# Four transformer layers and a fifth block on one core: eight more up-projection chunks per layer in the wide form, and the gate-value product issued behind the next chunk's additions

## The chip, the cores and the metric

The kernel runs on one core of a Trainium2 chip. TensorE (PE) multiplies, with its weight loads shown apart (PEld); VectorE (DVE), ScalarE (ACT) and GpSimd (POOL) do the elementwise work; SyncE (SP) issues the transfers of the weights. The metric is the device time of one execution in microseconds (us), lower is better.

## The reference

All of it is in float32 on a sequence of 256 tokens with 1024 channels. Four layers have an attention (three kinds) and a gated feed-forward network with a causal convolution of width 3 on both halves of the hidden tensor. A fifth block has another mixer and a network whose convolution is on the gate half alone.

```python
def conv_gated_ffn(h, w_up, conv_w, conv_b, w_down):      # layers 0 to 3, D_FF = 2752
    u = h @ w_up
    u = lax.conv_general_dilated(u, conv_w[:, None, :], ..., padding=[(CONV_W - 1, 0)],
                                 feature_group_count=C) + conv_b
    gate, val = jnp.split(u, 2, axis=-1)
    return (jax.nn.silu(gate) * val) @ w_down

def conv_ffn(h, w_up, conv_w, conv_b, w_down):            # the fifth block, D_FF_2 = 2816
    gate, val = jnp.split(h @ w_up, 2, axis=-1)
    ...                                                   # convolution of width 3 on gate
    return (jax.nn.gelu(conv, approximate=True) * val) @ w_down
```

## The kernel before

**Splitting for precision.** A matmul operand is kept as two parts of the type fp32r, high and low. A product is made of three: high weight by high activation, high weight by low activation, low weight by high activation. In `h_both` and `act_both` the high and the low part of an activation tile lie side by side (256 columns each).

**Weights.** SyncE brings the weights in 241 pieces of 1 MB (128 x 2048) into the three buffers of `w_raw` (line 392); piece n+3 is issued once the low part of piece n is made. ScalarE writes the high part into one of five slots, `w_hi` (the cast of line 411), and VectorE the low part, `w_lo` (the subtraction of line 957). A chunk of the up projection uses one piece. TensorE waits for the low part of its chunk's piece (`lo_ready`) and for its banks (`bank_free`).

**The up stage.** It has 22 chunks, numbered 0 to 21; a chunk makes 128 gate channels (bank `pj[slot]`) and 128 value channels (bank `val_bank[slot]`) for all 256 tokens, with three slots that are used in turn, so that TensorE can start chunk c+3 once the banks of chunk c are free. Chunks 0 to 2 follow the norm of the layer and are made in a form of their own. From chunk 3 on a chunk is *narrow* or *wide* (table `WIDE_UP`, line 73):

- narrow: per channel tile and per 128 input channels three matmuls of 256 columns (lines 1787 to 1789), 48 in a chunk, all summed in columns 0 to 255 of the bank;
- wide: one matmul of the low weight by 256 columns (line 1799) and one of the high weight by high and low activation together, 512 columns (line 1802), 32 in a chunk. The part of the low activation ends up in columns 256 to 511 of the bank, and the two halves have to be added.

Chunks 10 to 19 of layers 0 to 3 are wide, and chunks 2 to 21 of the fifth block. Chunk 21 of layers 0 to 3 has half the channels (`half_step`).

**The work behind a chunk**, in the order in which each engine issues it, narrow chunk j of layers 0 to 3:

- ScalarE: two activations that start the convolution, scale and bias, from the banks to `cgate` and `cval` (slices of `tmp`, line 890); the high part of the piece of chunk j+4 or j+5 (line 411); silu of the gate (line 894), which waits for three of VectorE's taps.
- VectorE: four taps of the convolution (line 1544), `tmp` plus a weight times a shifted source; the low part of a piece (line 957), of chunk j+3 up to chunk 3, of chunk j+4 from chunk 4 on, so that chunk 4 has two of them; the product of gate and value (line 1564), which waits for the silu.
- GpSimd: the cast of the product to the high part of `act_both` (line 1759) and the subtraction that leaves the low part (line 1762).

In a narrow chunk the taps read the bank. In a wide chunk ScalarE first copies the right halves of both banks to `tmp` (line 875), VectorE adds them to the left halves into `u_sb` (line 1536, two additions; the second frees the banks), and the activations and taps read `u_sb`. In the fifth block there is one activation, two taps, and the product is on line 1569.

**The down stage** begins on TensorE with the hidden tiles 0 to 18 of its first two output tiles, 76 matmuls, for which those tiles must be ready; then it waits for all hidden tiles and for a cast of ScalarE (line 907) that moves the half tile 21 to where the matmul needs it. The half tile comes from VectorE's product of line 1493 and GpSimd's cast and subtraction behind it.

Of the kernel before, what the change touches and what calls it, by code (L numbers as in the profile page):

```python
# [37 lines left out]
FT = 22  # L38
RING = 3
# [32 lines left out]
RAW = 3  # L72
WIDE_UP = (range(10, 20),) * 4 + (range(2, FT),)
UNITS = STD // P
# [25 lines left out]
def build(nc, xT, w_std, params, consts, lam, onehot, tables, pT, out):  # L100
    ctx = ExitStack()
    with ctx:
# [67 lines left out]
        bank_free = sem("bank_free")  # L170
# [114 lines left out]
        def wide_count(ffn, j):  # L285

            return sum(len(WIDE_UP[f]) for f in range(ffn)) + j - WIDE_UP[ffn][0] + 1

# [30 lines left out]
        def slot_of(c0, k):  # L319
            return (c0 + k) % RING  # L320
# [624 lines left out]
        def _(dve):  # L945
# [291 lines left out]
            for kind, c0, n in STAGES:  # L1237
# [188 lines left out]
                elif kind == "wo":  # L1426
# [54 lines left out]
                    app += 1  # L1481
                elif kind == "up":
                    def half_step(j, c, slot):
                        at = j * 8 + PARAM["conv"] + ffn * FT * 8
                        dve.wait_ge(conv_init, (j + ffn * FT) * 2 + 2)
                        dve.scalar_tensor_tensor(cgate[:, slot, 1:S], pj[slot][:, 0:S - 1], par[:, at + 1:at + 2],
# [9 lines left out]
                    def step(j, c, slot, split):  # L1496
# [45 lines left out]
                        def tap(v, lag):  # L1542
# [4 lines left out]
                                ALU.mult, ALU.add)  # L1547

                        for v in range(convs):
                            dve.wait_ge(conv_init, init + (v + 1))  # L1550
                            tap(v, 1).then_inc(conv_part, 1)
# [5 lines left out]
                        split()  # L1557
                        dve.wait_ge(gated, n_ + 1)
                        if convs == 2:
                            if wide:  # L1560
                                dve.wait_ge(wide_taps, wide_count(ffn, j))
                            else:
                                dve.wait_ge(bank_free, c + (RING + 1))
                            dve.tensor_tensor(cval[:, slot, :], cgate[:, slot, :], cval[:, slot, :],  # L1564
                                              ALU.mult).then_inc(prod_done, 1)
                        else:
                            if wide:
# [4 lines left out]
                            else:  # L1572
                                product.then_inc(bank_free, 1)
                                dve.wait_ge(bank_free, c + (RING + 1))
                                dve.memset(wait_mark[:, 0:1], 0.0).then_inc(prod_done, 1)

                    for j in range(n):
                        step(j, c0 + j, slot_of(c0, j), lambda: split_to(weights_of(layer, c0 + j) + low_up(j)))
                    ffn += 1
                elif kind == "down":  # L1580
# [1005 lines left out]
```

## Time and profile before

| | us |
|---|---|
| median of 3 runs | 1475.66 |
| lowest, highest | 1474.86, 1477.33 |
| profiled execution, its own time | 1474.86 |
| its span in the trace | 1472.9 |

Share of the span in which each engine is busy: PE 100%, PEld 92%, DVE 76%, ACT 63%, POOL 23%. The granted TensorE clock is at its full level in all forty slices of the page. A busy span of TensorE overstates its work, since matmuls overlap; for the length of a stretch the starts of its matmuls are to be read, and what could hold it up is to be read on the other engines. In a timeline, instructions of one line are merged: the second number is the time from the start of the first to the end of the last.

### The profile page before, as it was taken

What the parts mean: (1) busy time and instruction counts of PE and PEld (TensorE: products, weight loads), DVE (VectorE), ACT (ScalarE), POOL (GpSimd) and SP (SyncE); (2) the same over time, 40 slices, a digit from 0 to 9 for tenths busy, and PEclk for the clock granted to TensorE, in tenths of its full rate; (3) what the DMA queues carried; (4) which work ended last, traced back from release to release, by engine and by line L of the source; (5) the groups of instructions that cost most, each with busy time, mean ns of one, the idle gap of its engine ahead of it and who ended that gap; (6) DMA issues with size and microseconds to landing.
All of it is one profiled execution on the core that took longest, in us unless ns stands there. A gap on an engine that the chain in (4) does not pass through costs nothing.

```text
span 1472.9 us, 26512 instructions
## 1 busy us (share of the span) xinstructions
PE 1466.7 (100%) x10440; PEld 1357.9 (92%) x10440; DVE 1119.5 (76%) x1885; ACT 926.6 (63%) x1536; POOL 331.5 (23%) x461
## 2 busy tenths in 40 slices
PE   9999999999999999999999999999999999999998
PEld 8999989899999898989989899999898999988888
DVE  7778898565578995787899566688995688798655
ACT  7776666456756674575676456766664558566453
POOL 2104212211132222212322221023212271022100
PEclk9999999999999999999999999999999999999999
DMA  8644656444335565562565546545655464356560
GB/s 277 202 165 138 222 197 223 168 162 162 115 134 206 204 204 196 175 199 79 204 206 199 199 159 198 160 134 210 204 196 193 165 213 175 109 206 206 176 222 32
DMA packets 39687, 265.03 MB, mean 180 GB/s; under 512 B 5247, under 2 KB 5562, under 8 KB 8976
## 3 DMA queue, kind: packets, MB, share of 16 engines
q1 hardware_dynamic: 36432, 255.54, 49.9%
q0 software_dynamic: 2992, 7.79, 2.2%
q8 instruction: 82, 1.34, 0.4%
q14 instruction: 37, 0.30, 0.1%
q10 hardware_dynamic: 144, 0.05, 0.0%
HBM read 262.24 MB, written 1.12 MB: 179 GB/s over the span
## 4 chain that ended last, share of the span: by engine, by line
PE 98%; ACT 1%; DVE 1%; DMA 1%; issue 0%; SPq 0%; ACTq 0%
PE bank L1802 29%; PE bank L1799 14%; PE bank L1787 13%; PE bank L1788 13%; PE bank L1789 13%; PE bank L1850 6%; PE bank L1859 3%; PE bank L2034 1%; PE bank L2023 1%; PE bank L2015 1%; PE bank L2014 1%; DMA w_raw<-w_std 1%; PE bank L2394 1%; PE bank L2035 1%; PE bank L2087 0%; PE bank L2209 0%
## 5 line engine op out<-in xcount | busy, mean ns | idle before, releaser
L957 DVE TENSOR_TENSOR w_lo<-w_raw,w_hi 128x2048 fp32r<-128x2048 f32 x239 | 549.5, 2307 | 74.4 <-ACT w_hi L411 74.3
L411 ACT CAST w_hi<-w_raw 128x2048 fp32r<-128x2048 f32 x239 | 452.7, 1903 | 82.7 <-DMA w_raw<-w_std 62.4
L1802 PE MATMUL bank<-h_both,w_hi 128*128 128x512 f32 x960 | 301.5, 395 | 0.0
L1787 PE MATMUL bank<-h_both,w_hi 128*128 128x256 f32 x992 | 284.3, 287 | 0.0
L1788 PE MATMUL bank<-h_both,w_hi 128*128 128x256 f32 x992 | 280.6, 283 | 0.0
L1789 PE MATMUL bank<-h_both,w_lo 128*128 128x256 f32 x992 | 280.5, 283 | 0.0
L1802 PE MATMUL bank<-act_both,w_hi 128*128 128x512 f32 x848 | 267.4, 395 | 0.0
L1799 PEld LDWEIGHTS bank<-h_both,w_lo 128*128 128x128 f32 x960 | 179.9, 188 | 42.4 <-DVE w_lo L957 0.3
L1787 PEld LDWEIGHTS bank<-h_both,w_hi 128*128 128x128 f32 x992 | 189.9, 191 | 4.0 <-issue 2.8
L1788 PEld LDWEIGHTS bank<-h_both,w_hi 128*128 128x128 f32 x992 | 190.0, 192 | 0.4
L1789 PEld LDWEIGHTS bank<-h_both,w_lo 128*128 128x128 f32 x992 | 190.0, 192 | 0.0
L1799 PE MATMUL bank<-h_both,w_lo 128*128 128x256 f32 x960 | 188.7, 278 | 0.0
L1799 PEld LDWEIGHTS bank<-act_both,w_lo 128*128 128x128 f32 x848 | 157.2, 188 | 34.2
L1799 PE MATMUL bank<-act_both,w_lo 128*128 128x256 f32 x848 | 170.1, 278 | 0.0
L1759 POOL CAST act_both<-tmp 128x256 f32 x110 | 53.9, 490 | 438.4 <-DVE tmp L1564 319.3
L1802 PEld LDWEIGHTS bank<-h_both,w_hi 128*128 128x128 f32 x960 | 146.2, 189 | 0.0
L1802 PEld LDWEIGHTS bank<-act_both,w_hi 128*128 128x128 f32 x848 | 130.7, 189 | 1.7
L1544 DVE SCALAR_TENSOR_TENSOR tmp<-u_sb,par,tmp 128x255 f32<-128x255 f32 x234 | 115.4, 536 | 21.7 <-ACT tmp L890 20.9
L1850 PE MATMUL bank<-h_both,w_hi 128*128 128x256 f32 x400 | 106.8, 289 | 0.2 <-DVE w_lo L1143 0.2
L1850 PE MATMUL bank<-h_both,w_lo 128*128 128x256 f32 x400 | 104.5, 283 | 0.0
L1787 PE MATMUL bank<-act_both,w_hi 128*128 128x256 f32 x340 | 99.2, 292 | 0.0
L1788 PE MATMUL bank<-act_both,w_hi 128*128 128x256 f32 x340 | 96.1, 283 | 0.0
(236 smaller groups left out, 2549.7 us busy)
## 6 DMA issues: line engine op xcount, KB each, us to landing
w_raw<-w_std SPq DMA_DIRECT2D x239, 1024.0 KB, 4.9
act_both<-vec_dram POOLq DMA_DIRECT2D x56, 128.0 KB, 3.4
w_raw<-w_std SPq DMA_DIRECT2D x3, 512.0 KB, 8.5
x<-xT SPq DMA_DIRECT2D x2, 512.0 KB, 5.5
out<-x SPq DMA_DIRECT2D x3, 256.0 KB, 2.1
w_raw<-w_std SPq DMA_DIRECT2D x2, 256.0 KB, 4.9
par<-params SPq DMA_DIRECT2D x1, 446.0 KB, 6.6
cst<-consts SPq DMA_DIRECT2D x1, 256.0 KB, 9.4
```

The source lines that it names most:

```text
L411: act.copy(w_hi[:, n % SLOTS, :], w_raw[:, n % RAW, :]).then_inc(hi_ready, 1)
L957: dve.tensor_tensor(w_lo[:, n % SLOTS, :], w_raw[:, n % RAW, :], w_hi[:, n % SLOTS, :].bitcast(F32), ALU.subtract).then_inc(lo_ready, 1)
L1544: return dve.scalar_tensor_tensor(to[:, slot, lag:S], source(v)[:, 0:S - lag], par[:, bass.ds(at + (4 * v + 2 - lag), 1)], to[:, slot, lag:S],
L1759: pool.tensor_copy(act_hi[:, bass.ds(j, 1), :].squeeze(1) if not isinstance(j, int) else act_hi[rows, j, :], cval[rows, slot, :]).then_inc ...
L1787: pe.matmul(dst, wh, xh, start=first, stop=False, skip_group_check=shared)
L1788: pe.matmul(dst, wh, xl, start=False, stop=False, skip_group_check=shared)
L1789: done = pe.matmul(dst, wl, xh, start=False, stop=last, skip_group_check=shared)
L1799: pe.matmul(bank[:, 0:S], weights[k][1], moving[k][0], start=start and k == 0, stop=False, skip_group_check=True)
L1802: done = pe.matmul(bank[:, :], weights[k][0], moving[k][1], start=False, stop=stop and k == len(weights) - 1, skip_group_check=True)
L1850: pe.matmul(dst, a, b, start=k == 0 and w is wh and (n == 0 or not shared), stop=False, skip_group_check=shared)
L1859: done = pe.matmul(dst, a, b, start=False, stop=k == DT - 1, skip_group_check=shared)
L2014: pe.matmul(into[m][:, 0:QB], q[:, 0:QB], k[:, 0:QB], start=True, stop=True)
```

## The change

The table makes chunks 3 to 9 and chunk 20 of layers 0 to 3 wide too (18 wide chunks a layer, where there were 10), and the product of chunk j is no longer issued on VectorE at the end of chunk j but in chunk j+1, behind the scaling of a first chunk or the two additions of a wide one and ahead of the taps. The last one is issued ahead of the half chunk's taps, or after the stage. This holds for all chunks of layers 0 to 3 and for chunk 0 and the wide chunks of the fifth block. ScalarE's and GpSimd's code is as it was; what a wide chunk needs there follows from the table.

```diff
-WIDE_UP = (range(10, 20),) * 4 + (range(2, FT),)
+WIDE_UP = (range(3, FT - 1),) * 4 + (range(2, FT),)
...
                 elif kind == "up":
+                    later = []
+
+                    def multiply_later():
+
+                        if later:
+                            later.pop()()
+
                     def half_step(j, c, slot):
                         at = j * 8 + PARAM["conv"] + ffn * FT * 8
+                        multiply_later()
                         dve.wait_ge(conv_init, (j + ffn * FT) * 2 + 2)
...
+                        multiply_later()
                         for v in range(convs):
                             dve.wait_ge(conv_init, init + (v + 1))
                             tap(v, 1).then_inc(conv_part, 1)
...
                         split()
-                        dve.wait_ge(gated, n_ + 1)
-                        if convs == 2:
...
+                        def multiply():
+
+                            dve.wait_ge(gated, n_ + 1)
+                            if convs == 2:
+                                if wide:
+                                    dve.wait_ge(wide_taps, wide_count(ffn, j))
+                                else:
+                                    dve.wait_ge(bank_free, c + (RING + 1))
+                                dve.tensor_tensor(cval[:, slot, :], cgate[:, slot, :], cval[:, slot, :],
+                                                  ALU.mult).then_inc(prod_done, 1)
+                                return
...
+                        if convs == 2 or first or wide:
+                            later.append(multiply)
+                        else:
+                            multiply()
+
                     for j in range(n):
                         step(j, c0 + j, slot_of(c0, j), lambda: split_to(weights_of(layer, c0 + j) + low_up(j)))
+                    multiply_later()
```

VectorE's instructions in layer 0 from the taps of chunk 3 to the product of chunk 4, before (L1544 are the taps, L957 the low part of a weight piece, L1564 the product):

```order
226 L1544 SCALAR_TENSOR_TENSOR tmp<-bank,par,tmp 128x255 x2
227 L1544 SCALAR_TENSOR_TENSOR tmp<-bank,par,tmp 128x254 x2
228 L957 TENSOR_TENSOR w_lo<-w_raw,w_hi 128x2048
229 L1564 TENSOR_TENSOR tmp<-tmp 128x256
230 L1544 SCALAR_TENSOR_TENSOR tmp<-bank,par,tmp 128x255 x2
231 L1544 SCALAR_TENSOR_TENSOR tmp<-bank,par,tmp 128x254 x2
232 L957 TENSOR_TENSOR w_lo<-w_raw,w_hi 128x2048 x2
233 L1564 TENSOR_TENSOR tmp<-tmp 128x256
```

The same place in the changed kernel, from the additions of chunk 3 to the two low parts of chunk 4 (there L1544 are the additions, L1576 the product, L1552 the taps):

```order
225 L1544 TENSOR_TENSOR u_sb<-bank,tmp 128x256 x2
226 L1576 TENSOR_TENSOR tmp<-tmp 128x256
227 L1552 SCALAR_TENSOR_TENSOR tmp<-u_sb,par,tmp 128x255 x2
228 L1552 SCALAR_TENSOR_TENSOR tmp<-u_sb,par,tmp 128x254 x2
229 L957 TENSOR_TENSOR w_lo<-w_raw,w_hi 128x2048
230 L1544 TENSOR_TENSOR u_sb<-bank,tmp 128x256 x2
231 L1576 TENSOR_TENSOR tmp<-tmp 128x256
232 L1552 SCALAR_TENSOR_TENSOR tmp<-u_sb,par,tmp 128x255 x2
233 L1552 SCALAR_TENSOR_TENSOR tmp<-u_sb,par,tmp 128x254 x2
234 L957 TENSOR_TENSOR w_lo<-w_raw,w_hi 128x2048 x2
```

Two additions have come in, the taps read `u_sb` and `tmp` instead of a bank and `tmp`, and the product (of the chunk before) stands between the additions and the taps.

VectorE at the end of the stage, from the taps of chunk 20 to the last low part ahead of the down stage, before (L1486 and L1489 are the half chunk's taps, L1493 its product):

```order
304 L1544 SCALAR_TENSOR_TENSOR tmp<-bank,par,tmp 128x255 x2
305 L1544 SCALAR_TENSOR_TENSOR tmp<-bank,par,tmp 128x254 x2
306 L957 TENSOR_TENSOR w_lo<-w_raw,w_hi 128x2048
307 L1564 TENSOR_TENSOR tmp<-tmp 128x256
308 L1486 SCALAR_TENSOR_TENSOR tmp<-bank,par,tmp 128x255
309 L1489 SCALAR_TENSOR_TENSOR tmp<-bank,par,tmp 128x254
310 L957 TENSOR_TENSOR w_lo<-w_raw,w_hi 128x2048
311 L1493 TENSOR_TENSOR tmp<-tmp 64x256
312 L957 TENSOR_TENSOR w_lo<-w_raw,w_hi 128x2048
```

And in the changed kernel (L1494, L1497 and L1501 for the half chunk):

```order
310 L1544 TENSOR_TENSOR u_sb<-bank,tmp 128x256 x2
311 L1576 TENSOR_TENSOR tmp<-tmp 128x256
312 L1552 SCALAR_TENSOR_TENSOR tmp<-u_sb,par,tmp 128x255 x2
313 L1552 SCALAR_TENSOR_TENSOR tmp<-u_sb,par,tmp 128x254 x2
314 L957 TENSOR_TENSOR w_lo<-w_raw,w_hi 128x2048
315 L1576 TENSOR_TENSOR tmp<-tmp 128x256
316 L1494 SCALAR_TENSOR_TENSOR tmp<-bank,par,tmp 128x255
317 L1497 SCALAR_TENSOR_TENSOR tmp<-bank,par,tmp 128x254
318 L957 TENSOR_TENSOR w_lo<-w_raw,w_hi 128x2048
319 L1501 TENSOR_TENSOR tmp<-tmp 64x256
320 L957 TENSOR_TENSOR w_lo<-w_raw,w_hi 128x2048
```

From the product of chunk 20 on the order is the same as before; ahead of it the additions and the product of chunk 19 have come in.

## Rows read from the trace of the kernel before

**Rows 1.** Page, chain of work that ended last: share of the span by engine.

```profile
PE 98%; ACT 1%; DVE 1%; DMA 1%; issue 0%; SPq 0%; ACTq 0%
```

**Rows 2.** Timeline, TensorE, layer 0: start us, duration us, instruction; chunks 3, 10, 20 begin.

```profile
141.01 0.28 PE L1787 MATMUL bank<-h_both,w_hi 128*128 128x256 f32 x1
...
181.33 0.40 PE L1799 MATMUL bank<-h_both,w_lo 128*128 128x256 f32 x2
...
237.07 0.28 PE L1787 MATMUL bank<-h_both,w_hi 128*128 128x256 f32 x1
```

**Rows 3.** Timeline, VectorE, layer 0: chunk 4 (narrow), chunks 8 to 9 (narrow), chunk 10 (wide).

```profile
158.93 1.71 DVE L1544 SCALAR_TENSOR_TENSOR tmp<-bank,par,tmp 128x255 f32<-128x255 f32 x4
160.57 4.48 DVE L957 TENSOR_TENSOR w_lo<-w_raw,w_hi 128x2048 fp32r<-128x2048 f32 x2
...
178.32 0.42 DVE L1564 TENSOR_TENSOR tmp<-tmp 128x256 f32<-128x256 f32 x1
...
182.42 0.42 DVE L1564 TENSOR_TENSOR tmp<-tmp 128x256 f32<-128x256 f32 x1
...
187.51 0.76 DVE L1536 TENSOR_TENSOR u_sb<-bank,tmp 128x256 f32<-128x256 f32 x2 [0.58 <-ACT tmp L875]
188.61 1.76 DVE L1544 SCALAR_TENSOR_TENSOR tmp<-u_sb,par,tmp 128x255 f32<-128x255 f32 x4 [0.34 <-ACT tmp L890]
190.29 2.29 DVE L957 TENSOR_TENSOR w_lo<-w_raw,w_hi 128x2048 fp32r<-128x2048 f32 x1
```

**Rows 4.** Timeline, ScalarE: chunks 3 and 10 of layer 0, then chunk 3 of layer 1.

```profile
156.23 1.91 ACT L411 CAST w_hi<-w_raw 128x2048 fp32r<-128x2048 f32 x1 [3.59 <-DMA w_raw<-w_std]
158.04 0.41 ACT L894 ACTIVATE tmp<-tmp 128x256 f32<-128x256 f32 x1
...
187.11 0.65 ACT L875 COPY tmp<-bank 128x256 f32<-128x256 f32 x2 [1.47 <-PE bank L1802]
...
456.68 1.91 ACT L411 CAST w_hi<-w_raw 128x2048 fp32r<-128x2048 f32 x1 [4.78 <-DMA w_raw<-w_std]
```

**Rows 5.** Timeline of layer 1, a wide chunk: VectorE, then GpSimd.

```profile
503.60 0.41 DVE L1564 TENSOR_TENSOR tmp<-tmp 128x256 f32<-128x256 f32 x1
503.93 0.74 DVE L1536 TENSOR_TENSOR u_sb<-bank,tmp 128x256 f32<-128x256 f32 x2
505.01 1.94 DVE L1544 SCALAR_TENSOR_TENSOR tmp<-u_sb,par,tmp 128x255 f32<-128x255 f32 x4 [0.34 <-ACT tmp L890]
506.88 2.28 DVE L957 TENSOR_TENSOR w_lo<-w_raw,w_hi 128x2048 fp32r<-128x2048 f32 x1
...
504.18 0.40 POOL L1759 CAST act_both<-tmp 128x256 f32 x1 [4.17 <-DVE tmp L1564]
504.76 0.74 POOL L1762 TENSOR_TENSOR act_both<-tmp,act_both 128x256 f32 x1 [0.18 <-POOL act_both L1759]
```

**Rows 6.** Timeline, VectorE and GpSimd, two other places where both work from SBUF.

```profile
142.50 2.28 DVE L957 TENSOR_TENSOR w_lo<-w_raw,w_hi 128x2048 fp32r<-128x2048 f32 x1
...
144.70 2.14 DVE L1544 SCALAR_TENSOR_TENSOR tmp<-u_sb,par,tmp 128x255 f32<-128x255 f32 x4
...
142.69 2.69 POOL L1762 TENSOR_TENSOR act_both<-tmp,act_both 128x256 f32 x1 [0.19 <-POOL act_both L1759]
...
311.88 1.85 DVE L1003 SCALAR_TENSOR_TENSOR tmp<-x,par,rstd 128x256 f32<-128x256 f32 x2
...
311.35 2.09 POOL L1652 TENSOR_TENSOR h_both<-tmp,h_both 128x256 fp32r<-128x256 f32 x2 [16.50 <-ACT h_both L461]
```

**Rows 7.** Timeline, end of layer 0's up stage: VectorE, GpSimd, ScalarE, TensorE.

```profile
247.46 0.41 DVE L1564 TENSOR_TENSOR tmp<-tmp 128x256 f32<-128x256 f32 x1
...
251.91 2.40 POOL L1759 CAST act_both<-tmp 64x256 fp32r<-64x256 f32 x1 [2.55 <-DVE tmp L1493]
...
255.15 0.40 ACT L907 CAST act_both<-act_both 64x256 fp32r<-64x256 f32 x1 [3.39 <-POOL act_both L1762]
...
258.94 0.40 PE L1799 MATMUL bank<-act_both,w_lo 128*128 128x256 f32 x2
```

More of the change, by code:

```diff
@@ L1557, in step @@
                         split()
-                        dve.wait_ge(gated, n_ + 1)
-                        if convs == 2:
[L1560 to L1566, printed above, removed]
+                        def multiply():
[8 more added lines that the diff above has]
+                                return
                             if wide:
```

## The prediction, on record before the changed kernel ran

> **What bounds the kernel now.** I read the chain of waits first: 98% of it is TensorE [rows 1], so a change gains what it takes off TensorE and loses what it makes TensorE wait for. Then the starts of the matmuls in layer 0's up stage: chunks 3 to 9, narrow, last from 141.01 to 181.33, 5.76 us each; chunks 10 to 19, wide, from 181.33 to 237.07, 5.574 us each [rows 2]. A wide chunk is 0.186 us shorter.
>
> Next the engines behind it. In a narrow chunk VectorE needs 4.10 us where nothing makes it wait (product to product, 178.32 to 182.42 [rows 3]); TensorE needs 5.76. This spare 1.66 us a chunk is used: the stage starts with a backlog. TensorE ends chunk 4 at 141.01 + 2 x 5.76 = 152.5, VectorE takes it up at 158.93 [rows 3], 6.4 us later. At chunk 10 the backlog is gone: TensorE ends it at 186.90 (181.33 + 5.574), ScalarE copies at 187.11 [rows 4], VectorE adds at 187.51 [rows 3]. So **the narrow chunks are where VectorE catches up**, and they are what the change removes.
>
> **The gain on TensorE.** Eight chunks by 0.186 us is 1.49 us a layer, 5.95 us in four layers, as long as VectorE, ScalarE and the weights keep pace.
>
> **VectorE's time for a wide chunk, without GpSimd.** First addition to first tap 1.10 us (187.51 to 188.61), four taps 1.68 us to the start of the low part (190.29) [rows 3]; the low part 2.20 us to the next instruction (two take 4.48, one 2.28 [rows 3, 5]). Together 4.98. The product (0.33 us from its start to the next, 503.60 to 503.93 [rows 5]) came on top before and now falls into the wait of 0.34 us ahead of the first tap. By this sum the moved product saves 0.33 us, and a backlog would shrink by 0.6 us a chunk.
>
> **What the moved product runs into.** GpSimd starts on a product 0.58 us after it starts (504.18), and subtracts 0.58 us later (504.76), for 0.74 us [rows 5]. Three places show that such an instruction and a VectorE instruction with both inputs in SBUF don't run together. In layer 1 the first tap of a wide chunk comes during the subtraction, and the taps need 1.87 us (505.01 to 506.88 [rows 5]) instead of 1.68. In rows 6 a subtraction that begins 0.19 us into a low part lasts 2.69 us: the low part ends at 144.78, the subtraction at 145.38, 0.60 later; the four taps behind it span 2.14 us, against 1.71 for four that read a bank [rows 3]. And at 311.88 two taps of the norm's kind take 1.85 us together while GpSimd has two subtractions: GpSimd gets in between two VectorE instructions that stand back to back [rows 6]. Additions and narrow taps read a bank, and the narrow taps stand where GpSimd's work on the chunk before falls, yet take 1.71 [rows 3]; I count them as spared.
>
> Before, the 1.9 us after a product fell on additions and a wait (wide) or on bank taps (narrow). Now the product stands 0.67 us behind the first addition, so the cast comes at +1.25 and the subtraction at +1.83 to +2.6, and the four taps at +1.10 to +2.8: **both meet SBUF taps in every wide chunk**. The cast lies beside the first tap and delays the second by about 0.03 us. The subtraction gets in at a boundary between taps, keeps the port for 0.60 us, and the tap behind it ends 0.28 us after it (144.70 + 0.96 where the subtraction ended at 145.38; that 0.28 is my estimate from the two spans in rows 6); two taps that start 0.40 us apart are then 0.92 apart: +0.52. A wide chunk takes VectorE 4.98 + 0.55 = **5.53 us**, against TensorE's 5.574. Bounds: 4.98 if nothing collides, 5.7 if both get in separately and fully (0.26 + 0.52). I take 5.53, the value by rows 5 and 6. At 5.53 a backlog of 8 us stays for the whole stage.
>
> The Trainium skill, "SBUF — State Buffer", in the section with the single rule on ports, says that VectorE and GpSimd share one pair of SBUF ports as an exclusive lock: an instruction of VectorE with two SBUF inputs and one of GpSimd that reads SBUF block each other for their whole length. Rows 5 and 6 agree. By its "whoever starts first keeps it" alone, a subtraction could cost the taps its full 0.74 us, some 0.2 more a chunk than I take.
>
> **The backlog at the start.** In layer 0 ScalarE casts at 156.23, as before, since that waits for a transfer; it is issued behind the low part of chunk 2, which moves little. Silu of chunk 3 at 158.04 [rows 4], copies of chunk 4 at 158.35, additions 0.40 behind (187.11 to 187.51) at 158.75, first tap 159.85, the two low parts from 162.1 to 166.5 (1.68 + 0.55, then 2 x 2.20). The low part for chunk 7 is ready at 162.1 + 2.28 = 164.4; TensorE, 4 x 5.574 after 141.01, wants it at 163.3. So it **waits 1.1 us at chunk 7**, which eats most of the 1.49. Additions of chunk 5 at 166.5.
>
> **The end of the stage.** 15 chunks later, 15 x 5.53 = 83.0, additions of chunk 20 at 249.5; its product, now behind its low part, 5.53 later at 255.0. Before, that product was at 247.46 and the last cast ended at 255.15 + 0.40 = 255.55, 8.1 us later, with the same instructions between [rows 7]. I add 0.1 for a subtraction caught behind a low part: 255.0 + 8.2 = 263.2. TensorE needs this cast for hidden tiles 19 to 21; it took them up at 258.94 without a wait [rows 7], 3.4 us of cover. Now it starts them at 263.2: **+4.2 us in layer 0**, with the gain and the wait at chunk 7 in it, since this end is set by VectorE alone. On the way the down stage also begins late, as tile 18's product waits for chunk 19's additions; that wait is inside the 4.2.
>
> Layers 1 to 3 have the same program and the same start, so 4 x 4.2 = 16.8. In the fifth block only the product moves; two taps, then a low part, and VectorE has time there; I count -0.1 for a product less ahead of chunk 7. **Sum: +16.7 us.** The profiled execution took 1474.86 (span 1472.9); against the median 1475.66 that gives **1492.4 us**, +1.1%.
>
> One unknown: in layer 1 the cast of rows 4 stands at 456.68, 1.3 us later, counted from chunk 3, than in layer 0. Before, the narrow chunks absorbed it. Now such a late piece moves VectorE's whole stage: +1.2 us in each layer that has one, 0 to 4.8 in all. I count none, and put it in the range.
>
> **Rivals.**
> (a) *No collision that matters*: GpSimd's work finds room beside the taps or is held behind the low part. VectorE 5.0 us a chunk, the backlog is gone by chunk 20, gain 1.49 less 0.5 at chunk 7 or nothing: -1.0 to -1.5 a layer, **1470 us**. For it: the moved product does fill a real wait. Against it: three places in the rows. Faster.
> (b) *Half of it*: VectorE at 5.3. The end comes 15 x 0.23 = 3.4 us earlier, +0.8 a layer, **1479 us**. The point from which the sign turns is 5.25 us a chunk.
> (c) *Late pieces in the first chunks of most layers*, or 5.6 us a chunk: **1497 to 1500 us**. TensorE's clock stays at its level by the page; a wait of 3 us in each layer might change that, and I have no row for it.
> (d) *ScalarE, not VectorE, is late*: by rows 4 the copies take 0.65, a cast 1.91 and the silu 0.41, and the scaling between copies and first tap is shorter than the 1.10 between addition and tap [rows 3]: at most 4.1 of 5.57, so I give it nothing of its own.
>
> **How the numbers follow.** Forecast 64%, (a) 10%, (b) 13%, (c) 13%. The forecast's own spread, 4.2 ± 0.8 a layer, is 1489 to 1496. The range takes in half of (b) and most of (c): 1481 to 1498. This kernel's measurement tells 0.2% (3 us) from no change: faster 0.10 by (a); same 0.06, the low part of (b); slower 0.84.
>
> **What would show it.** In the changed profile: wide chunks on TensorE at 5.57 us; a gap of about 1 us at chunk 7; VectorE with additions 5.5 us apart from chunk 5 to 20, never waiting for the copies; one of the last three taps near 1 us long in each chunk; taps from `u_sb` with a mean well over 0.48; a wait of TensorE for ScalarE's cast of line 907, near 3 us in four places, and about 1 us at the start of the down stage. The prediction is wrong if taps stay at 0.48 us, or if VectorE waits for the copies in the middle of the stage.

## The result

The changed kernel takes 1501.22 us (median of 5 runs, 1500.75 to 1502.49), the kernel before 1475.66: ratio 1.0174, 95% interval 1.0163 to 1.0185. It is slower, as forecast, but by 26 us instead of 16.7, and outside the range of 1481 to 1498. The ratios below leave out one slow execution each of the kernels no_defer (7300.79 us) and defer_only (2889.83 us), which the medians given for these two include (without them 1496.15 and 1475.78 us).

### The profile page after: what moved, and what is told of

It is laid out like the page before. It is cut to its first block, busy times and chain, and to the rows that moved or that the text cites. A ratio compares the mean times of both kernels' runs of the same rounds, so it can differ in the third digit from the quotient of the medians.

```text
span 1499.6 us, 25616 instructions
## 1 busy us (share of the span) xinstructions
PE 1471.7 (98%) x9928; PEld 1336.8 (89%) x9928; DVE 1181.5 (79%) x1949; ACT 943.0 (63%) x1600; POOL 367.8 (25%) x461
## 3 DMA queue, kind: packets, MB, share of 16 engines
q8 instruction: 78, 1.28, 0.3%
## 4 chain that ended last, share of the span: by engine, by line
PE 67%; DVE 23%; issue 6%; DMA 2%; ACT 1%; POOL 0%; SPq 0%; POOLq 0%; ACTq 0%
PE bank L1820 18%; DVE tmp L1552 11%; PE bank L1817 9%; PE bank L1805 9%; PE bank L1806 8%; PE bank L1807 8%; DVE w_lo L957 6%; PE bank L1868 5%; DVE u_sb L1544 3%; PE bank L1877 3%; DMA w_raw<-w_std 2%; DVE tmp L1576 2%; PE bank L2052 1%; PE bank L2041 1%; PE bank L2033 1%
## 5 line engine op out<-in xcount | busy, mean ns | idle before, releaser
L957 DVE TENSOR_TENSOR w_lo<-w_raw,w_hi 128x2048 fp32r<-128x2048 f32 x239 | 553.4, 2323 | 74.5 <-ACT w_hi L411 74.4
L1820 PE MATMUL bank<-h_both,w_hi 128*128 128x512 f32 x1472 | 462.3, 395 | 0.0
L1817 PEld LDWEIGHTS bank<-h_both,w_lo 128*128 128x128 f32 x1472 | 275.9, 188 | 69.7 <-DVE w_lo L957 5.2
L1817 PE MATMUL bank<-h_both,w_lo 128*128 128x256 f32 x1472 | 289.7, 278 | 3.4 <-DVE w_lo L957 3.4
L1820 PEld LDWEIGHTS bank<-h_both,w_hi 128*128 128x128 f32 x1472 | 224.1, 189 | 0.0
L1552 DVE SCALAR_TENSOR_TENSOR tmp<-u_sb,par,tmp 128x255 f32<-128x255 f32 (+1 forms) x362 | 206.3, 605 | 3.0 <-ACT tmp L890 0.8
L1817 PE MATMUL bank<-act_both,w_lo 128*128 128x256 f32 x848 | 174.6, 285 | 17.7 <-issue 12.7
L890 ACT ACTIVATE tmp<-u_sb,par 128x256 f32<-128x256 f32 x181 | 100.3, 596 | 137.6 <-DVE u_sb L1544 132.2
L1777 POOL CAST act_both<-tmp 128x256 f32 x110 | 70.2, 639 | 433.4 <-DVE tmp L1576 345.2
L1805 PE MATMUL bank<-h_both,w_hi 128*128 128x256 f32 x480 | 139.2, 290 | 0.0
L1806 PE MATMUL bank<-h_both,w_hi 128*128 128x256 f32 x480 | 135.7, 283 | 0.0
L1807 PE MATMUL bank<-h_both,w_lo 128*128 128x256 f32 x480 | 135.6, 283 | 0.0
L1780 POOL TENSOR_TENSOR act_both<-tmp,act_both 128x256 f32 x110 | 109.5, 996 | 19.2 <-POOL act_both L1777 18.8
L1868 PE MATMUL bank<-h_both,w_hi 128*128 128x256 f32 x400 | 106.8, 289 | 0.9 <-DVE w_lo L1143 0.8
L1868 PE MATMUL bank<-h_both,w_lo 128*128 128x256 f32 x400 | 104.5, 283 | 0.0
L1807 PE MATMUL bank<-act_both,w_lo 128*128 128x256 f32 x340 | 96.1, 283 | 0.0
```

The source lines that it names most:

```text
L890: act.activation(to[:, slot, :], source, ACT.Identity, bias=col(3), scale=col(2)).then_inc(conv_init, 1)
L957: dve.tensor_tensor(w_lo[:, n % SLOTS, :], w_raw[:, n % RAW, :], w_hi[:, n % SLOTS, :].bitcast(F32), ALU.subtract).then_inc(lo_ready, 1)
L1552: return dve.scalar_tensor_tensor(to[:, slot, lag:S], source(v)[:, 0:S - lag], par[:, bass.ds(at + (4 * v + 2 - lag), 1)], to[:, slot, lag:S],
L1777: pool.tensor_copy(act_hi[:, bass.ds(j, 1), :].squeeze(1) if not isinstance(j, int) else act_hi[rows, j, :], cval[rows, slot, :]).then_inc ...
L1780: pool.tensor_tensor(act_lo[rows, j, :], cval[rows, slot, :], act_hi[rows, j, :].bitcast(F32), ALU.subtract).then_inc(act_free, 1)
L1805: pe.matmul(dst, wh, xh, start=first, stop=False, skip_group_check=shared)
```

## The profile after

**The chain.** Of the chain of work that ended last 23% is now VectorE, where it was 1% [rows 1]:

```profile
PE 67%; DVE 23%; issue 6%; DMA 2%; ACT 1%; POOL 0%; SPq 0%; POOLq 0%; ACTq 0%
```

**TensorE in layer 0**, timeline as in rows 2 (start us, duration, instruction, in brackets the idle time before it and what ended it): chunk 7, then the first matmuls of the down stage, then two more like the second row, 4 us later.

```profile
165.39 0.50 PE L1817 MATMUL bank<-h_both,w_lo 128*128 128x256 f32 x2 [1.01 <-DVE w_lo L957]
...
251.50 0.77 PE L1817 MATMUL bank<-act_both,w_lo 128*128 128x256 f32 x2 [4.93 <-DVE w_lo L957]
252.06 1.05 PE L1820 MATMUL bank<-act_both,w_hi 128*128 128x512 f32 x2
...
256.12 0.63 PE L1820 MATMUL bank<-act_both,w_hi 128*128 128x512 f32 x2
```

Two things stand here that the rows of before don't have. TensorE waits 1.01 us at chunk 7 and 4.93 us ahead of the down stage, both times for a **low part of weights** (VectorE's line 957). And behind the long wait two matmuls of 512 columns last 1.05 us together, where 4 us later they last 0.63.

**The granted clock** tells why. Windows of layer 0 around the start of the down stage, then one of layer 1, from the start of its down stage to the return of the clock (from:to, length, busy time and instructions of PE, PEld, DVE, ACT, POOL, granted clock, DMA share, GB/s):

```profile
245.00:251.50 6.50, 1.57 (x15) 1.40 (x13) 6.48 (x10) 3.72 (x6) 1.30 (x2) 1.00 0.42 163
251.50:254.00 2.50, 2.50 (x8) 2.21 (x9) 2.48 (x6) 2.24 (x3) 1.26 (x2) 0.50 0.66 170
254.00:256.00 2.00, 2.00 (x10) 1.73 (x10) 2.00 (x3) 1.42 (x3) 0.06 (x1) 0.79 0.74 311
256.00:260.00 4.00, 4.00 (x26) 3.52 (x25) 3.96 (x5) 3.67 (x4) 1.14 (x2) 1.00 0.43 147
...
556.25:562.05 5.80, 5.80 (x19) 5.03 (x20) 5.78 (x10) 3.65 (x5) 1.31 (x2) 0.50 0.53 184
```

0.50 is the lower of the two levels, 1.2 GHz instead of 2.4. TensorE had done nothing for 4.9 us before, and for 4.2 to 4.3 us in layers 1 to 3. In 2.5 us it gets through 8 matmuls, at the full level through 16. The down stages of layers 0 to 3 run at 0.50 for their first 3.35, 5.80, 6.05 and 5.02 us, 20.2 us in all; at half the rate that is up to 10.1 us lost. The Trainium skill, "TensorE: Matmul & The Clock Gate", Part 1, says that the array's clock is passed at half or at full rate and falls to half when the engine idles. The windows agree: 0.50 and 1.00, with 0.79 only in the window in which it changes. The page of the profile, in tenths and fortieths of the span, shows 9 throughout; only short windows show this.

**VectorE and GpSimd in a wide chunk** (timelines of the changed kernel, a wide chunk of layer 0, as rows 5 show one of layer 1 before):

```profile
184.80 0.74 DVE L1544 TENSOR_TENSOR u_sb<-bank,tmp 128x256 f32<-128x256 f32 x2
185.47 0.41 DVE L1576 TENSOR_TENSOR tmp<-tmp 128x256 f32<-128x256 f32 x1
185.89 2.34 DVE L1552 SCALAR_TENSOR_TENSOR tmp<-u_sb,par,tmp 128x255 f32<-128x255 f32 x4
188.15 2.28 DVE L957 TENSOR_TENSOR w_lo<-w_raw,w_hi 128x2048 fp32r<-128x2048 f32 x1
190.35 0.74 DVE L1544 TENSOR_TENSOR u_sb<-bank,tmp 128x256 f32<-128x256 f32 x2
...
186.04 0.59 POOL L1777 CAST act_both<-tmp 128x256 f32 x1 [4.05 <-DVE tmp L1576]
186.81 0.75 POOL L1780 TENSOR_TENSOR act_both<-tmp,act_both 128x256 f32 x1 [0.18 <-POOL act_both L1777]
```

The four taps span 2.34 us, where they spanned 1.76 without a collision [rows 3], and a chunk takes 5.55 us (184.80 to 190.35), with no wait in it. Of the four taps one carries the difference (durations in ns: lowest, median, highest):

```profile
L1552 DVE SCALAR_TENSOR_TENSOR tmp<-u_sb,par,tmp x4: 469/504/1003, 185.9 to 187.8; 128x255 f32<-128x255 f32 x2, 128x254 f32<-128x254 f32 x2
```

**Where the 26.7 us lie.** The starts of the matmuls give the time that each stretch lost (+) or gained against the profiled execution before, in us. "Up" is from the start of chunk 3 to the first matmul of the down stage, "down" from there to chunk 3 of the next layer. The last column, from the start of the span to chunk 3 of layer 0, differs by up to 4 us between these profiled executions, all of it ahead of chunk 0, in code that no kernel here changes. Each row is one execution, so small differences between rows prove nothing; the medians rest on several.

| kernel | up, layers 0, 1, 2, 3 | down, layers 0, 1, 2, 3 | fifth block | ahead |
|---|---|---|---|---|
| changed | 4.90, 3.78, 3.81, 3.99 | 1.58, 2.70, 2.83, 2.39 | -0.16 | 0.90 |
| no_defer | 3.14, 2.78, 2.90, 2.98 | 1.53, 1.57, 2.63, 2.69 | -0.15 | 2.37 |
| defer_only | 0.00, 0.08, -0.16, 0.00 | 0.0 each | -0.02 | 4.00 |
| busy_pe | 5.03, 6.33, 6.05, 6.54 | 0.34, 0.0, 0.0, 0.0 | -0.16 | 1.06 |
| split16 | 2.19, 0.84, 0.80, 1.18 | 3.25, 3.27, 3.31, 3.27 | -0.14 | 1.09 |
| late | 1.38, 0.60, 0.51, 0.86 | 1.68, 1.65, 1.69, 1.66 | -0.16 | 1.28 |
| late_split | 2.11, 0.53, 0.67, 0.96 | 1.67, 1.68, 1.68, 1.66 | -0.15 | 0.81 |
| late_first16 | -1.30, -1.54, -1.52, -1.20 | 2.46, 1.55, 1.60, 1.56 | -0.15 | 1.94 |
| order_before_7 | 0.04, -0.15, 1.15, 1.20 | 0.31, 0.35, 0.34, 1.67 | -0.08 | 2.65 |
| order_before_8 | -0.56, -0.76, -0.08, -0.56 | 0.0, 0.0, 0.33, 0.0 | -0.15 | 0.15 |
| late_6_first16 | -0.93, -1.13, -1.11, -0.93 | 0.50, 0.66, 0.67, 0.52 | -0.15 | 1.75 |
| late_7_split | -0.74, -0.92, -0.92, -0.46 | 0.0, 0.09, 0.0, 0.09 | -0.15 | 1.40 |

In the changed kernel the up stages with the waits cost 16.5 us, the down stages **9.5 us** more, although nothing waits in them.

## Experiment 1: one half of the change at a time

**no_defer** is the kernel before with

```diff
-WIDE_UP = (range(10, 20),) * 4 + (range(2, FT),)
+WIDE_UP = (range(3, FT - 1),) * 4 + (range(2, FT),)
```

> Chunks 3 to 20 wide in layers 0 to 3, the product left where it stood before the change (behind its own chunk's low part). My theory: the loss comes from taking VectorE's catch-up time away, the moved product only adds to it. VectorE's wide chunk in the old order is about 5.48 us when it has a backlog (layer 1 of the kernel before) against 5.54 in the changed kernel, and its stage ends about 1.2 us earlier a layer. The up stage with the wait at its end costs +3.1 us a layer against before; the wait ahead of the down stage is about 3.3 us instead of 4.4 to 5.1. If a wait of 3.3 us lowers TensorE's clock as that of 4.4 us does, 1.6 to 2.8 us a layer more, less 0.4 of cover: 1475.7 + 12.4 + 7 = 1495 us; if not, 1488 us. The rival, that the moved product is what loses, expects 1470 to 1478 us here.

**defer_only** is the changed kernel with that line turned back.

> The product moved behind the next chunk's additions, chunks 10 to 19 wide as before the change. My theory: each wide chunk still has VectorE waiting for ScalarE's copies of TensorE's result, so the tap that collides with the subtraction takes 1.0 instead of 0.48 us and the end of the stage stays: 1475 us, with the waits of 0.2 us at chunk 7 of layers 1 and 2 and of the fifth block gone. The rival, that the collision by itself costs TensorE time, expects +1 us a layer, 1480 us.

no_defer: 1496.55 us, ratio 1.0135 (1.0115 to 1.0156). defer_only: 1476.20 us, ratio 0.9999 (0.9989 to 1.001). So the wide chunks lose, and the moved product adds 0.9 to 1.8 us a layer to the up stage where VectorE is behind, and nothing where it is not. In no_defer the wait ahead of the down stage is shorter, and the clock falls all the same (TensorE's timeline, then the window behind it):

```profile
251.21 0.77 PE L1799 MATMUL bank<-act_both,w_lo 128*128 128x256 f32 x2 [3.57 <-issue]
...
251.20:253.20 2.00, 1.99 (x7) 1.81 (x8) 1.66 (x5) 1.39 (x3) 1.13 (x2) 0.50 0.55 111
```

## Experiment 2: is it the clock?

**busy_pe**, the changed kernel with work for TensorE inside the wait (18 matmuls whose result nobody uses):

```diff
                     early = FT - 3
+                    if layer < 4:
+                        pe.wait_ge(act_free, RING + ffn * FT + 1)
+                        pe.wait_ge(bank_free, c0 + 1)
+                        for _ in range(18):
+                            pe.matmul(pj[slot_of(c0, 0)][:, :], act_hi[:, 0, 0:P],
+                                      act_both[:, 0, :, :].rearrange("p a b -> p (a b)"),
+                                      start=True, stop=True, skip_group_check=True)
                     pe.wait_ge(act_free, RING + ffn * FT + early)
```

> The changed kernel with 18 matmuls of 128x512 (4.2 us by 0.232 each) on TensorE ahead of each down stage of layers 0 to 3, inside the wait, on an activation tile that is complete and into the bank that the down stage clears; their result isn't used. My theory: the granted clock fell to 0.50 for 3 to 5.6 us because TensorE stood idle for 4.4 to 5.1 us; kept busy, it stays at 1.00, the down stage begins at the same time and runs 1.6 to 2.8 us faster, and then about 0.5 us a layer of waiting for ScalarE's last cast appears: 1501.2 - 9.5 + 2 = 1493.7 us. The rival, that the down stage is slower for another reason (weights, contention, or a throttle on load), expects 1501 us or more, and a clock under 1.00 again behind the added matmuls.

The windows of the same places (columns as above; 246 to 251.8 holds the added matmuls):

```profile
246.00:251.80 5.80, 4.93 (x24) 3.72 (x23) 5.78 (x10) 3.74 (x6) 1.32 (x2) 1.00 0.51 182
251.80:254.00 2.20, 2.20 (x13) 1.94 (x14) 2.18 (x6) 1.94 (x3) 0.97 (x2) 1.00 0.64 130
...
557.80:560.00 2.20, 2.20 (x14) 1.90 (x14) 2.19 (x5) 2.20 (x3) 1.26 (x2) 1.00 0.72 294
```

The clock stays at 1.00, and the down stages lose 0.35 us in all instead of 9.5. Layer 0 is the clean comparison: its down stage begins when the low part is ready, as in the changed kernel, and loses 0.34 us instead of 1.58. With the 20.2 us at half the rate above, **the 9.5 us are the clock's**; a reason in the weights or in contention is out, since those are as in the changed kernel. Yet the kernel takes 1499.69 us (ratio 1.0159, 1.0141 to 1.0177), 6 us above the 1493.7 I expected, since the up stages of layers 1 to 3 now lose 6.1 to 6.5 us each instead of 3.8 to 4.0. ScalarE's cast that waits for the piece of chunk 8 and TensorE at chunk 7 show one part of it, in layer 1, with the window behind:

```profile
463.05 1.91 ACT L411 CAST w_hi<-w_raw 128x2048 fp32r<-128x2048 f32 x1 [2.88 <-DMA w_raw<-w_std]
...
471.25 0.79 PE L1817 MATMUL bank<-h_both,w_lo 128*128 128x256 f32 x2 [2.15 <-DVE w_lo L957]
...
471.20:473.00 1.80, 1.75 (x6) 1.56 (x7) 1.80 (x1) 0.00 (x0) 0.00 (x0) 0.50 0.51 86
```

In the changed kernel the same cast waited 1.54 us:

```profile
462.66 1.91 ACT L411 CAST w_hi<-w_raw 128x2048 fp32r<-128x2048 f32 x1 [1.54 <-DMA w_raw<-w_std]
```

This is the late piece of rival (c): counted from chunk 3 the cast is 1.34, 0.96 and 1.40 us later in layers 1, 2 and 3 than in the changed kernel. In layer 1 the wait at chunk 7 grows from 0.80 to 2.15 us and the clock falls there too, so TensorE ends chunk 21 2.85 us later. But VectorE's low part, which the down stage needs, is only 1.35 us later. The other part is the end of the stage (TensorE, then VectorE):

```profile
553.75 4.27 PE L2423 MATMUL bank<-act_both 128*128 128x512 f32 x18
557.86 0.40 PE L1817 MATMUL bank<-act_both,w_lo 128*128 128x256 f32 x2
...
554.27 2.28 DVE L957 TENSOR_TENSOR w_lo<-w_raw,w_hi 128x2048 fp32r<-128x2048 f32 x1
```

The low part is ready at 556.55, but TensorE, which came late, works on the added matmuls until it begins the down stage at 557.86, with no wait. So of the 2.2 to 2.6 us that each of these layers loses more, 0.9 to 1.4 are the late piece, near the 1.2 us at which I had priced it, and the other 1.2 to 1.3 are the experiment's own: the added matmuls outlast the wait that they were to fill. The fall of the clock at chunk 7 costs only by way of them. The added matmuls gave 9 us back in the down stages; the late pieces took 3.7 us and the overrun 3.7.

What makes a piece late was not tried. Executions of one kernel differ (busy_pe's four took 1495.70 to 1501.17 us). While the late piece of layer 1 is under way, between 456 and 464 us, a transfer of instructions is too (DMA view: queue, packets, MB, share); the changed kernel has none there.

```profile
q8 instruction: 1, 0.02, 0.7%
```

In the up stages of all thirteen traces, 473 transfers of a piece have neither another piece nor such a transfer of 16 KB beside them, and none of them takes more than 5.3 us from issue to landing. Of 182 with a transfer of instructions beside them some take up to 6.3 us, though the median is 4.9. So it goes with the late pieces, but does not always make one, and that it is the cause was only seen side by side, not tried.

## Experiment 3: what the down stage stood for

**split16**, the changed kernel with

```diff
-                    for f in range(2):
-                        down(f, 0, early)
+                    down(0, 0, UNITS)
+                    down(0, UNITS, early)
+                    down(1, 0, early)
```

> The changed kernel with the first sum of the down stage cut: hidden tiles 0 to 15, which need one piece of weights, then tiles 16 to 18, which need the second. My theory: the down stage stood for the low part of the second piece (behind chunk 19's taps on VectorE), not for tile 18's product as I predicted. So here TensorE takes up the down stage at once behind chunk 21, about 5 us earlier, waits about 3 us at the second output tile (third piece) and about 1.5 us for the last cast; the end is set by that cast. Without a fall of the clock 1493 us, with one at the 3 us wait 1496 to 1501 us. The rival (tile 18's product is what it stood for) expects the first wait to stay at 2 us or more ahead of tile 16.

1493.46 us, ratio 1.0122 (1.0105 to 1.0139). TensorE's timeline: the start of the down stage and the last wait in layer 1, the start in layer 0, and the windows behind the two starts.

```profile
552.46 0.50 PE L1817 MATMUL bank<-act_both,w_lo 128*128 128x256 f32 x2 [1.29 <-POOL act_both L1780]
...
568.88 0.50 PE L1817 MATMUL bank<-act_both,w_lo 128*128 128x256 f32 x2 [1.11 <-ACT act_both L907]
...
248.98 0.60 PE L1817 MATMUL bank<-act_both,w_lo 128*128 128x256 f32 x2 [2.30 <-POOL act_both L1780]
...
552.50:554.50 2.00, 2.00 (x12) 1.78 (x13) 2.00 (x3) 1.35 (x4) 0.00 (x0) 1.00 0.74 307
...
248.98:251.00 2.02, 2.02 (x7) 1.82 (x8) 2.02 (x3) 1.39 (x4) 0.00 (x0) 0.57 0.62 251
```

The long wait was for the second piece of weights: hidden tiles 0 to 18 need 19 of the blocks of which a piece holds 16. Its low part stands behind chunk 19's taps on VectorE. With that out of the way the wait that the prediction had forecast appears, for the subtraction of tile 18: 1.29 us. My expectation for this run had none there, 3 us for the third piece and 1.5 us for the cast. But my edit left the wait for tile 18 ahead of everything, so the rival of that text was half right. The long wait has become three of 1.29, 1.53 and 1.11 us; the clock stays at 1.00 in layers 1 to 3, and falls in layer 0, where the first is 2.30 us. **Layers 1 and 2 cost 4.11 us each**, where the changed kernel's cost 6.5 and 6.6 and I had forecast 4.2; layers 0 and 3 cost 5.4 and 4.5.

## Experiment 4: the collision

**late**, the changed kernel with the product behind the taps:

```diff
-                        multiply_later()
+                        if convs == 1:
+                            multiply_later()
                         for v in range(convs):
...
                             tap(1, 2).then_inc(wide_taps if wide else bank_free, 1)
+                        multiply_later()
                         split()
```

> The changed kernel, but the product of a chunk stands behind the next chunk's taps and ahead of its low part, instead of ahead of the taps (layers 0 to 3; the fifth block as in the changed kernel). My theory: in the changed kernel one tap in each wide chunk loses 0.52 us to the subtraction. Here GpSimd's cast falls on the low part and waits for its end, its subtraction then falls on additions that read a bank: no tap is hit, each of the four starts 0.40 us behind the one before, and VectorE's wide chunk is 4.98 + 0.33 = 5.31 us instead of 5.54 with a backlog. The stage ends 3.3 us earlier in each layer: the wait ahead of the down stage is about 2.1 us, +0.95 us a layer against before, so 1479.5 us if TensorE's clock stays at 1.00, up to 1487 us if that wait lowers it. The rival, that VectorE needs 5.5 us a wide chunk wherever the product stands, expects 1495 us or more.

1483.55 us, ratio 1.0051 (1.0036 to 1.0066), 17.7 us less than the changed kernel. VectorE, then GpSimd, timeline:

```profile
199.27 0.75 DVE L1544 TENSOR_TENSOR u_sb<-bank,tmp 128x256 f32<-128x256 f32 x2
200.37 1.76 DVE L1552 SCALAR_TENSOR_TENSOR tmp<-u_sb,par,tmp 128x255 f32<-128x255 f32 x4 [0.34 <-ACT tmp L890]
202.05 0.42 DVE L1578 TENSOR_TENSOR tmp<-tmp 128x256 f32<-128x256 f32 x1
202.38 2.29 DVE L957 TENSOR_TENSOR w_lo<-w_raw,w_hi 128x2048 fp32r<-128x2048 f32 x1
204.58 0.75 DVE L1544 TENSOR_TENSOR u_sb<-bank,tmp 128x256 f32<-128x256 f32 x2
...
202.63 2.29 POOL L1779 CAST act_both<-tmp 128x256 f32 x1 [2.09 <-DVE tmp L1578]
205.10 0.74 POOL L1782 TENSOR_TENSOR act_both<-tmp,act_both 128x256 f32 x1 [0.18 <-POOL act_both L1779]
```

A chunk takes 5.31 us, the forecast to the hundredth: the taps are back at 1.76, and the wait of 0.34 us that the change had filled is back too. It is GpSimd that pays: its cast stands for 2.29 us, until the low part has ended, instead of 0.40, and in this chunk nobody waits for it. In the changed kernel **filling a wait of 0.34 us cost 0.58 us of taps**. The Trainium skill, "SBUF — State Buffer", in the section "Who interferes with whom", calls this an exclusive lock, held by whoever starts first. The cast's 2.29 us agree. The changed kernel shows one thing more: between two taps that stand back to back the subtraction gets in, and the later tap lasts 1.00 us instead of 0.48.

The order before the change stands between the two, as **order_before_7** shows (VectorE, then GpSimd, timeline; chunks 7 to 20 wide): 5.51 us a chunk.

```profile
504.13 0.74 DVE L1536 TENSOR_TENSOR u_sb<-bank,tmp 128x256 f32<-128x256 f32 x2
505.22 1.96 DVE L1544 SCALAR_TENSOR_TENSOR tmp<-u_sb,par,tmp 128x255 f32<-128x255 f32 x4 [0.34 <-ACT tmp L890]
...
509.64 0.74 DVE L1536 TENSOR_TENSOR u_sb<-bank,tmp 128x256 f32<-128x256 f32 x2
...
504.97 0.74 POOL L1762 TENSOR_TENSOR act_both<-tmp,act_both 128x256 f32 x1 [0.18 <-POOL act_both L1759]
```

**late_split** has the edits of late and of split16.

> As the run late, with the first sum of the down stage cut at hidden tile 16. My theory: the down stage begins without a wait, the only wait left is 1.5 us for ScalarE's last cast, too short to lower the clock (waits of 1.2 to 1.6 us did not in the run split16); +0.4 us a layer, 1477.5 us, within 0.2% of before. The rival, that the wait ahead of the down stage was for something else than the second piece of weights, expects the time of the run late.

1484.81 us, ratio 1.0057 (1.0043 to 1.0071): a miss by 7 us. The waits of TensorE in `late` name the reason: not the weights, but the subtraction of tile 18, which the edit of split16 leaves ahead of everything. The numbers are the total, how many and the longest; the window is that behind the wait of 1.85 us in layer 1 of `late`.

```profile
PE bank L1819 <- POOL act_both L1782: 8.1, 4, 2.6
...
550.00:552.00 2.00, 1.97 (x7) 1.78 (x8) 1.99 (x6) 2.00 (x3) 0.00 (x0) 0.51 0.73 287
```

Executions of one kernel differ here: late_split's six took 1481.03 to 1486.86 us, with mean granted clocks from 1.000 (at 1482.04 us) to 0.994 (at 1486.86 us). The profiled one took 1486.14 us, has 0.995, and its clock falls in all four layers. So it seems to differ from one execution to the next whether these waits, 1.8 to 1.9 us in layers 1 to 3, cost the clock; a trace shows one execution.

**late_first16** puts that wait behind the first 16 tiles:

```diff
-                    pe.wait_ge(act_free, RING + ffn * FT + early)
-                    for f in range(2):
-                        down(f, 0, early)
+                    pe.wait_ge(act_free, RING + ffn * FT + UNITS)
+                    down(0, 0, UNITS)
+                    pe.wait_ge(act_free, RING + ffn * FT + early)
+                    down(0, UNITS, early)
+                    down(1, 0, early)
```

> As the run late_split, which missed its 1477.5 us: its wait of 1.8 us ahead of the down stage stayed, because TensorE there still waited for the subtraction of hidden tile 18 ahead of everything. Here it waits for tile 15's only, then takes 16 tiles, and waits for tile 18's behind them. My theory: down stage without a wait at its start, clock at 1.00, 1.5 us of waiting for ScalarE's last cast, +0.4 us a layer: 1477.5 us. The rival, that the moved product leaves the down stage's later parts as late as its first, expects 1482 us or more, with the wait and the clock of 0.50 at the second or third part.

1478.13 us, ratio 1.0019 (1.0009 to 1.0028). One wait above 0.25 us a layer is left, for ScalarE's last cast, in layer 0 the longest, and the clock behind it stays:

```profile
261.92 0.50 PE L1819 MATMUL bank<-act_both,w_lo 128*128 128x256 f32 x2 [1.67 <-ACT act_both L907]
...
261.92:264.00 2.08, 2.08 (x13) 1.90 (x14) 0.81 (x2) 0.00 (x0) 0.00 (x0) 1.00 0.94 398
```

So all eight chunks wide and the product moved, without the collision and without a fall of the clock, come out 2.6 us above the kernel before: the up stages gain 1.2 to 1.5 us a layer, and the down stages, with the wait for the cast, lose 1.6 to 2.5. What is left is the catch-up that is gone.

## Experiment 5: how many narrow chunks VectorE needs

Chunks 7 or 8 to 20 wide with nothing moved; then chunks 7 to 20 with the edits of late_split, and 6 to 20 with those of late_first16. The only further edit in each is the range.

> The kernel before with chunks 7 to 20 wide in layers 0 to 3 and nothing moved: against late_7_split this shows what the later place of the product is worth. My theory: in the old place the subtraction falls on the taps too, so VectorE's wide chunk is 5.48 us and four narrow chunks don't work its start off: a wait of 0.6 us ahead of the down stage, 0.4 us for the last cast, +0.3 us a layer and 1.4 us where a piece of weights comes late: 1477 us, up to 1481 us. The rival, that the number of wide chunks alone decides, expects 1472.5 us as late_7_split.

> The kernel before with chunks 8 to 20 wide in layers 0 to 3 and nothing moved. My theory: the narrow chunks 3 to 7 give VectorE back what it was behind, and the cover of 3.4 us at the end of the stage takes chunk 20: 3 x 0.186 = 0.56 us a layer where no piece of weights comes late, 0 where one does (layers 1 and 2 had one): 1474 us, not to be told from before. The rival, that any wide chunk more puts TensorE in a wait, expects 1478 us or more.

> As late_split, with chunks 7 to 20 wide only: chunks 3 to 6 stay narrow and let VectorE work off its start. My theory: no wait is left at chunk 7, nor at the down stage; four wide chunks more than before are 4 x 0.186 = 0.74 us a layer, 3.0 us: 1472.7 us, 0.2% faster. The rival, that a start of a stage like this also needs chunks 7 to 9 narrow, expects 1476 us or more.

> As late_first16, with chunks 6 to 20 wide and 3 to 5 narrow: the most wide chunks for which I expect nearly no wait. 5 x 0.186 = 0.93 us a layer gained, 0.1 us lost at ScalarE's last cast, up to 1.3 us where a piece of weights comes late: 1472.4 us (about that of late_7_split), 1475 us with two late pieces. A rival, that it gains the full 3.7 us, expects 1471.9 us and can't be told from this; the rival that three narrow chunks are too few expects 1476 us or more.

| kernel | us | ratio to before, interval |
|---|---|---|
| order_before_7 | 1481.20 | 1.0036 (1.0023 to 1.005) |
| order_before_8 | 1473.47 | 0.9987 (0.9978 to 0.9996) |
| late_7_split | 1472.27 | 0.9980 (0.9971 to 0.9989) |
| late_6_first16 | 1473.31 | 0.9983 (0.9974 to 0.9992) |

Three of the four came out within 1 us of their numbers. One wide chunk more, 7 instead of 8, turns a gain of 2 us into a loss of 5.5 in the order of before, while late_7_split, where the taps aren't hit, has the lowest median. It has two edits against order_before_7, the place of the product and the split at tile 16, so their 8.9 us are not shared out between the two. order_before_7 was expected at 1477 us, up to 1481, and came out at that end. Most of its loss is in layers 2 and 3, 1.2 us each in the up stage, and there a piece is late: in layer 2 the cast of rows 4, in layer 3 the one of 1030.29 below, 27.72 us behind chunk 3, where in layers 0 and 1 it stands at 26.67 and 26.56. So one narrow chunk less takes away the reserve that absorbed a late piece. In layer 3 the wait is also long enough to cost the clock, 1.3 us more in the down stage than in the other layers (ScalarE, TensorE and a window behind the wait):

```profile
1030.29 1.91 ACT L411 CAST w_hi<-w_raw 128x2048 fp32r<-128x2048 f32 x1 [5.43 <-DMA w_raw<-w_std]
...
1108.46 0.48 PE L1799 MATMUL bank<-act_both,w_lo 128*128 128x256 f32 x2 [1.79 <-issue]
...
1110.00:1112.00 2.00, 2.00 (x9) 1.71 (x8) 2.00 (x5) 2.00 (x3) 0.19 (x1) 0.50 0.89 373
```

The same trace has a longer wait behind which the clock stays, early in layer 0:

```profile
34.48 0.36 PE L1787 MATMUL bank<-h_both,w_hi 128*128 128x256 f32 x1 [1.93 <-DVE h_both L1182]
...
34.48:36.50 2.02, 2.02 (x18) 1.89 (x20) 1.76 (x10) 1.96 (x10) 1.10 (x2) 1.00 0.26 57
```

late_7_split has no wait above 0.13 us left between chunk 7 and the end of the down stages and is 3.4 us under the kernel before. Its interval overlaps those of order_before_8 and late_6_first16, so which of the three is best is open.

## Why the prediction was wrong, and where it was right

- *What bounds it*, right: the narrow chunks were VectorE's catch-up, and late_first16 shows that their loss alone outweighs the gain of 1.49 us a layer, if only by 2.6 us in all.
- *VectorE's 5.53 us a wide chunk*, right: 5.55 measured, by the mechanism named, a tap of 1.0 us in the middle. The 4.98 + 0.33 behind it is confirmed by the 5.31 of late. Rivals (a) and (b) fall.
- *The start*, right: additions of chunks 4 and 5 forecast at 158.75 and 166.5, measured 159.71 and 167.46, of which 0.90 is the later start; TensorE's wait at chunk 7 forecast 1.1, measured 1.01. A wait of VectorE for the copies of chunk 6 in layer 0, 0.62 us, was not foreseen: ScalarE made them behind a cast that waited 2.16 us for a transfer (first row below). It is most of what the up stage of layer 0 loses more than the others (4.90 us against 3.8 to 4.0).
- *The end*: the last cast ended at 264.54 + 0.41 = 264.95, forecast 263.2. Of the 1.75 us 0.90 is the start and 0.62 that wait.

```profile
171.16 1.92 ACT L411 CAST w_hi<-w_raw 128x2048 fp32r<-128x2048 f32 x1 [2.16 <-DMA w_raw<-w_std]
...
173.69 0.76 DVE L1544 TENSOR_TENSOR u_sb<-bank,tmp 128x256 f32<-128x256 f32 x2 [0.62 <-ACT tmp L875]
...
264.54 0.41 ACT L907 CAST act_both<-act_both 64x256 fp32r<-64x256 f32 x1 [4.19 <-POOL act_both L1780]
```

- *Where TensorE waits*, **wrong**: I had put about 1 us at the start of the down stage, for tile 18's product, and 3 us at the cast. I had not counted which pieces of weights its first matmuls need. Measured: 4.93 us at the start and none at the cast. The sum of the stage hardly changed by it, 16.5 us against 16.7, since VectorE's end sets it either way; but one wait of 4.9 us is not the same as several of 1 to 3.
- *The clock*, **the step that failed**: rival (c) says that a wait of 3 us "might change that, and I have no row for it", and the sum has nothing for it. It is 9.5 us, 1.6 to 2.8 in each of four layers, and busy_pe shows it, so this term left at nothing is the whole of the difference. No row of before has matmuls at the lower level, so its length could not be forecast, but the term could have stood in the sum with its unknown length, and the range could have been wider upward. With the 20.2 us at half rate that the changed kernel showed, it is 0 to 10.1 us, and the forecast would have been between 1492 and 1503 us.
- *Late pieces*, rival (c): in the changed kernel's trace the cast of rows 4 is on time in all four layers, and the one late transfer is that of 171.16. Where they came (busy_pe), they moved VectorE by 0.9 to 1.4 us, as priced.
- *The fifth block*: -0.16 us as forecast, but kernels without the moved product show it too, so it isn't the product's; its cause was not looked for.

## What to carry to other kernels

A time in which an engine other than the bound one is faster than it needs to be may be what repays a backlog; before it is filled, follow the backlog to the end of the stage and work out both orders of the two engines that share a port. Where a change makes the matmul engine wait, price the wait and then the clock behind it, and ask for every first matmul which weights it needs, not only which activations. Here three waits of 1.1 to 1.5 us cost less than one of 4.2 us (4.1 us a layer against 6.5). Work added to hold the clock must end before the wait does.

## What the runs showed of the hardware

- TensorE's clock fell to 0.50 behind waits of 4.93, 4.2 to 4.3, 3.57, 2.30, 2.15, 1.85 and 1.79 us, and stayed at 1.00 behind waits of 1.93, 1.67, 1.53, 1.29, 1.11 and 1.01 us. So between 1.8 and 1.9 us both were seen, and the length of the wait alone does not decide. It came back after some 3 to 6 us of matmuls, at a cost of 1.5 to 2.8 us behind the waits of 3.5 us and more, near half of that time. 18 matmuls whose result nobody uses were enough to hold it.
- GpSimd gets in between two instructions of VectorE that stand back to back (a tap of 1.00 us instead of 0.48), but stands behind one that has begun (cast of 2.29 us instead of 0.40).
- In the up stages a 1 MB piece of weights with no other piece beside it landed 4.6 to 5.3 us after its issue, and later than that, up to 6.3 us, only where a 16 KB transfer of instructions fell into it.
